# First modulation summed as columns, its last slot and the first w_in slot loaded in two parts, one MLP slot split around a norm

## Chip, cores and metric

The kernel runs on one core of one Trainium2 chip, as one program. The metric is the device time of an execution in microseconds (us); less is better. The profile is one execution, taken by the hardware profiler.

## What is computed

Two transformer blocks over 256 tokens (S) of width 1024 (D), all in float32. Only the first part is touched by the change:

```python
c_act = silu(c)                                  # 1 x 1024
mod = c_act @ w_ada + b_ada                      # 1 x 6144
sh1, sc1, g1, sh2, sc2, g2 = split(mod, 6)
h = rmsnorm(x, g[0]) * (1 + sc1) + sh1
y = token_mixer(h, w_in, w_out, sinks, bias)     # h @ w_in, attention, @ w_out
x = x + g1 * rmsnorm(y, g[1])
h = rmsnorm(x, g[2]) * (1 + sc2) + sh2
y = square(relu(h @ w1 + b1)) @ w2 + b2
x = x + g2 * rmsnorm(y, g[3])
...                                              # second block: mixer, then 16 experts
```

The second block ends with 16 experts, whose weights (w_gate, w_up, w_down, 24 MB an expert) are read once each.

## The kernel before, in words

Weights of everything ahead of the experts come through a ring of six slots of 1 MB (128 partitions x 2048 f32). `loads` lists them in order: eight slots of w_ada (`G_ADA0`, the columns of sh1 and sc1, slot k holding the rows p*8+k), nine of w_in (`G_WIN`), then w_out, the other w_ada slots, w1 and w2 (`G_MLP`), and the second block's. The sync queue (`block.sync`, L588) issues slot g when slot g-6 has been used; its semaphore is `loaded[g % 6]`. Other small loads stand in the same queue at fixed places: b_ada and b2 rows (L545, L547), the gain rows of w_ada (`load_gain`), the attention bias (L554). `tail_loaded` are three semaphores that the last unit of the last expert uses, hundreds of us later (L647, L1289). Experts' units of 4 MB go through a ring of five buffers laid over the same memory.

Order on every engine is written out by hand, and engines meet through semaphores.

The first modulation. `ada` (L776) takes one slot: four calls with `crep` (c_act of that slot, repeated to 32 columns) as the stationary operand and 512 columns of the slot as the moving one, each to its own 32 partitions of bank 2. So the sums lie in rows, one of 512 in each of four partition groups. After the third slot TensorE turns the eight 128x128 blocks of each of the two normalised token tiles (`turn_tiles`, through `turn`, L669); after the sixth, the rows of gains and biases and one product for the attention bias (L804). `turned_awake` (L733) are matmuls whose result nobody reads, two after each slot from the fourth on. VectorE copies the sums out in two halves (L1392), `turn_mod` (L785) turns them to columns with four calls, and `mod_columns` (L1375) adds b_ada; `fold_gain` multiplies the scale with the norm's gain. Then VectorE and ScalarE write the transposed, scaled and shifted tokens to `hT` (`place`; k 0 to 3 on VectorE, 4 to 7 on ScalarE, for tile 0, then tile 1).

The first w_in slot is used raw, in f32 (`raw_channels`, L745: 32 calls of 128x128 by 128 columns). All later slots are split: ScalarE writes a slot rounded to f32r (`round_slot`, L393), VectorE the rest (`residue_slot`, L403), both in two pieces, and the same is done to `hT` (`round_tile`, `residue_tile`, into `hR`). TensorE then takes three products of halves, in `both_still` (L722, L724) or `product` (L675 to L677).

Around the second norm (after w_out): x1 is summed per token tile (`first_sum`), ScalarE squares it (`root`, L1991), VectorE scales it (`norm_tile`, L1324), TensorE turns it, both place it. `G_MLP` is used raw, tile 0 then tile 1; `G_MLP + 1` is the first split slot. Before, both its pieces are rounded on ScalarE ahead of the square of tile 1 (L2118), and split on VectorE ahead of the norm of tile 1 (L1527).

## Time and profile before

| | us |
|---|---|
| median of 3 runs | 1452.87 |
| lowest and highest | 1452.32, 1454.32 |
| the profiled execution, device time | 1452.38 |
| its span (first to last instruction) | 1450.6 |
| TensorE busy (share) | 1060.3 (73%) |
| TensorE weight loads busy | 599.1 (41%) |
| VectorE, ScalarE, GpSimd busy | 425.8, 346.2, 85.8 |
| HBM read | 512.27 MB |

How to read it: the profiled execution's own time, 1452.38, is its span and 1.8 us around it. A line number (L787) is a line of the kernel; PE is TensorE, PEld its weight loads, DVE VectorE, ACT ScalarE, POOL GpSimd, SPq the queue of the sync engine that issues DMAs. A form such as 128x512 is partitions by elements. An f32 matmul call is recorded as two matmuls and two weight loads. "x8" is a count; what stands in brackets is the idle time before the group and what ended it. The times in a timeline start at the span's start.

### The profile page before, as it was taken

What the parts mean: (1) busy time and instruction counts of PE and PEld (TensorE: products, weight loads), DVE (VectorE), ACT (ScalarE), POOL (GpSimd) and SP (SyncE); (2) the same over time, 40 slices, a digit from 0 to 9 for tenths busy, and PEclk for the clock granted to TensorE, in tenths of its full rate; (3) what the DMA queues carried; (4) which work ended last, traced back from release to release, by engine and by line L of the source; (5) the groups of instructions that cost most, each with busy time, mean ns of one, the idle gap of its engine ahead of it and who ended that gap; (6) DMA issues with size and microseconds to landing.
All of it is one profiled execution on the core that took longest, in us unless ns stands there. A gap on an engine that the chain in (4) does not pass through costs nothing.

```text
span 1450.6 us, 15820 instructions
## 1 busy us (share of the span) xinstructions
PE 1060.3 (73%) x6734; PEld 599.1 (41%) x6734; DVE 425.8 (29%) x767; ACT 346.2 (24%) x600; POOL 85.8 (6%) x60
## 2 busy tenths in 40 slices
PE   6999999999999999766665565565545565655655
PEld 3866888888989985211211111121111121111111
DVE  3577776756979863000000000000000000000001
ACT  3566654636555942000000000000000000000001
POOL 1420059000000000000000000000000000000000
PEclk9999999999999999988888887788788878788788
DMA  9996468554564689999999999999999999999996
GB/s 362 338 376 205 147 230 262 191 186 146 175 232 125 261 342 418 431 431 430 428 432 432 432 431 430 432 431 430 429 431 432 433 433 428 431 429 431 433 432 279
DMA packets 83144, 514.50 MB, mean 355 GB/s; under 512 B 6659, under 2 KB 49134, under 8 KB 67330
## 3 DMA queue, kind: packets, MB, share of 16 engines
q1 hardware_dynamic: 82360, 512.68, 87.4%
q8 instruction: 53, 0.87, 0.3%
q10 hardware_dynamic: 490, 0.61, 0.1%
q0 software_dynamic: 224, 0.20, 0.0%
q14 instruction: 17, 0.14, 0.0%
HBM read 512.27 MB, written 1.07 MB: 354 GB/s over the span
## 4 chain that ended last, share of the span: by engine, by line
DMA 56%; PE 33%; DVE 7%; ACT 2%; issue 1%; SPq 1%; POOL 0%; DVEq 0%; ACTq 0%
DMA expert_ring<-in_w_up_e 20%; DMA expert_ring<-in_w_gate_e 18%; DMA expert_ring<-in_w_down_e 15%; PE PS L1255 6%; PE PS L675 5%; PE PS L677 5%; PE PS L676 5%; PE PS L722 4%; PE PS L724 2%; DVE wR L403 2%; PE PS L1294 2%; DMA ring<-in_w_in 1%; PE PS L749 1%; DMA ring<-in_w_ada 1%; ACT wR L393 1%
## 5 line engine op out<-in xcount | busy, mean ns | idle before, releaser
L1255 PE MATMUL PS<-expert_ring,xeT 128*32 128x512 f32 x2048 | 309.7, 761 | 225.9 <-DMA expert_ring<-in_w_up_e 124.0
L1255 PEld LDWEIGHTS PS<-expert_ring,xeT 128*32 128x32 f32 x2048 | 74.3, 135 | 458.1 <-issue 207.7
L1957 DVE TENSOR_TENSOR expert_rows<-expert_rows,PS 128x512 f32<-128x512 f32 x16 | 11.0, 687 | 805.6 <-PE PS L1255 805.6
L1294 PE MATMUL PS<-expert_ring,expert_rows 128*32 128x512 f32 x992 | 155.4, 777 | 103.7 <-DMA expert_ring<-in_w_down_e 101.4
L403 DVE TENSOR_TENSOR wR<-ring,wR 128x1024 fp32r<-128x1024 f32 x144 | 177.8, 1276 | 55.3 <-ACT wR L393 55.0
L393 ACT ACTIVATE wR<-ring 128x1024 fp32r<-128x1024 f32 x144 | 144.5, 1053 | 112.0 <-PE PS L677 110.8
L1294 PEld LDWEIGHTS PS<-expert_ring,expert_rows 128*32 128x32 f32 x992 | 38.7, 137 | 208.9 <-issue 119.5
L722 PE MATMUL PS<-hR,wR 128*128 128x512 f32 x320 | 112.2, 396 | 1.7 <-DVE wR L403 1.6
L724 PE MATMUL PS<-hR,wR 128*128 128x256 f32 x320 | 89.1, 278 | 0.0
L2332 ACT ACTIVATE selx<-PS 128x256 f32<-128x256 f32 x16 | 6.1, 384 | 322.4 <-PE PS L669 322.4
L675 PE MATMUL PS<-hR,wR 128*128 128x256 f32 x280 | 80.2, 286 | 0.8 <-DVE wR L403 0.8
L677 PE MATMUL PS<-hR,wR 128*128 128x256 f32 x280 | 79.2, 283 | 0.0
L676 PE MATMUL PS<-hR,wR 128*128 128x256 f32 x280 | 79.2, 283 | 0.0
L2327 ACT ACTIVATE expert_rows<-PS 128x512 f32<-128x512 f32 x16 | 9.6, 597 | 283.7 <-PE PS L1255 283.7
L2334 ACT ACTIVATE expert_rows<-PS 128x512 f32<-128x512 f32 x16 | 9.6, 597 | 257.0 <-PE PS L1294 257.0
L722 PEld LDWEIGHTS PS<-hR,wR 128*128 128x128 f32 x320 | 60.0, 188 | 16.5 <-issue 2.4
L724 PEld LDWEIGHTS PS<-hR,wR 128*128 128x128 f32 x320 | 60.2, 188 | 0.1
L675 PE MATMUL PS<-wR,hR 128*128 128x512 f32 (+1 forms) x144 | 55.7, 386 | 1.7 <-DVE wR L403 1.4
L677 PE MATMUL PS<-wR,hR 128*128 128x512 f32 (+1 forms) x144 | 54.3, 377 | 0.0
L676 PE MATMUL PS<-wR,hR 128*128 128x512 f32 (+1 forms) x144 | 54.3, 377 | 0.0
L675 PEld LDWEIGHTS PS<-hR,wR 128*128 128x128 f32 x280 | 53.7, 192 | 1.1 <-issue 1.0
L676 PEld LDWEIGHTS PS<-hR,wR 128*128 128x128 f32 x280 | 53.7, 192 | 0.0
(317 smaller groups left out, 1281.9 us busy)
## 6 DMA issues: line engine op xcount, KB each, us to landing
expert_ring<-in_w_down_e SPq DMA_DIRECT2D x30, 4096.0 KB, 44.2
expert_ring<-in_w_up_e SPq DMA_DIRECT2D x30, 4096.0 KB, 43.1
expert_ring<-in_w_gate_e SPq DMA_DIRECT2D x29, 4096.0 KB, 43.2
ring<-in_w SPq DMA_DIRECT2D x32, 1024.0 KB, 6.1
ring<-in_w_in SPq DMA_DIRECT2D x31, 1024.0 KB, 5.7
ring<-in_w_ada SPq DMA_DIRECT2D x16, 1024.0 KB, 12.8
ring<-in_w_out SPq DMA_DIRECT2D x8, 1024.0 KB, 10.6
expert_ring<-in_w_gate_e SPq DMA_DIRECT2D x4, 2048.0 KB, 12.4
```

The lines of the kernel that those rows point to most:

```text
L393: nc.scalar.activation(halves(g, 0)[:, piece], slot(g)[:, piece], ACT.Copy).then_inc(slot_rounded, 1)
L403: by.tensor_tensor(halves(g, 1)[:, piece], slot(g)[:, piece], halves(g, 0)[:, piece], ALU.subtract)\
L675: nc.tensor.matmul(o, first[0], second[0], start=start, stop=False, skip_group_check=onto)
L676: nc.tensor.matmul(o, first[0], second[1], start=False, stop=False, skip_group_check=onto)
L677: return nc.tensor.matmul(o, first[1], second[0], start=False, stop=stop, skip_group_check=onto)
L722: nc.tensor.matmul(o.rearrange("p (a s) -> p a s", a=2), w[0][:, k, cols], hR[:, :, k, :], start=(k == 0), stop=False, skip_group_check=True)
L724: mm = nc.tensor.matmul(o[:, 0:S], w[1][:, k, cols], hR[:, 0, k, :], start=False, stop=(k == KD - 1), skip_group_check=True)
L749: mm = nc.tensor.matmul(PS[:, bank, m * S + t * P:m * S + (t + 1) * P], k8(g)[:, k, m * P:(m + 1) * P], hT[:, k, t * P:(t + 1) * P], start ...
L1255: mm = nc.tensor.matmul(PS[32 * j:32 * j + 32, kind // 2, :], xeT[:, e // GROUP % 2, k, own], w[:, j // 2, j % 2, :, :], start=(k == 0), s ...
L1294: mm = nc.tensor.matmul(PS[32 * at:32 * at + 32, 3, :], hidT[:, c % 4, 2 * q + c // 4, :], w[c][:, 512 * half:512 * (half + 1)], start=(q ...
L1957: V.tensor_tensor(hid[:, :], silu[:, :], PS[:, 1, :], ALU.mult).then_inc(hid_set, 1)
L2327: N.activation(silu[:, :], PS[:, 0, :], ACT.Silu).then_inc(silu_set, 1)
```

## The change

1. `ada` is replaced for the first eight slots by `ada_columns`: the slot is the stationary operand, 16 blocks of 128x128, and c_act of that slot (one column) the moving one, into 16 columns of bank 2, summed over the eight slots. The copies to `modrow`, `turn_mod` for the first modulation and the `turned_awake` inside the loop go; `mod_columns` reads bank 2. The second modulation keeps its row form.
2. The eighth w_ada slot is loaded in two halves, with `tail_loaded[0]` for the first; the wait at the end of the kernel counts on from there.
3. The first w_in slot is loaded in two halves (k 0 to 3 and 4 to 7), and TensorE takes half by half, both token tiles of the first half first.
4. `G_MLP + 1`: the first piece is rounded and split ahead of tile 1's norm, the second behind it; VectorE places tile 1 ahead of splitting the tokens of tile 0.

```diff
@@ the sync queue
+                if g == G_ADA0 + 7:
+                    sp.dma_start(slot(g)[:, 0:D], ada_rows[7, :, 0:D]).then_inc(tail_loaded[0], 16)
+                    sp.dma_start(slot(g)[:, D:2 * D], ada_rows[7, :, D:2 * D]).then_inc(loaded[g % RING_P], 16)
+                    continue
+                if g == G_WIN:
+                    sp.dma_start(k8(g)[:, 0:4, :], src[:, 0:4, :]).then_inc(tail_loaded[1], 16)
+                    sp.dma_start(k8(g)[:, 4:8, :], src[:, 4:8, :]).then_inc(loaded[g % RING_P], 16)
+                    continue
                 sp.dma_start(dst(g), src).then_inc(loaded[g % RING_P], 16)
@@ TensorE
+            def ada_columns(k):
+
+                for c in range(2 * KD):
+                    if k == 7 and c == 0:
+                        pe.wait_ge(tail_loaded[0], 16)
+                    elif c == (KD if k == 7 else 0):
+                        arrived(pe, G_ADA0 + k)
+                    mm = nc.tensor.matmul(PS[:, 2, c:c + 1], slot(G_ADA0 + k)[:, c * P:(c + 1) * P], cact[:, k:k + 1],
+                                          start=(k == 0 and c == 0), stop=(k == 7), skip_group_check=True)
+                mm.then_inc(slots_used, 1)
 
             pe.wait_ge(crep_set, 1)
             for k in range(8):
-                ada(G_ADA0 + k, k, 2)
+                ada_columns(k)
...
-                if k >= 3:
-                    turned_awake(2)
 
             pe.wait_ge(bias_row_set, 1)
-            for part in range(2):
-                pe.wait_ge(modrow_set, part + 1)
-                turn_mod(0, 3, range(2 * part, 2 * part + 2))
             turned_awake(2)
-            arrived(pe, G_WIN)
-            for t in range(NT):
-                mm = raw_channels(G_WIN, 0, t, T1)
+            for half in range(2):
+                if half == 0:
+                    pe.wait_ge(tail_loaded[1], 16)
+                else:
+                    arrived(pe, G_WIN)
+                for t in range(NT):
+                    for j in range(4):
+                        pe.wait_ge(placed[half], placed_by(T1, t, j))
+                        k = 4 * half + j
+                        for m in range(2):
+                            mm = nc.tensor.matmul(PS[:, 0, m * S + t * P:m * S + (t + 1) * P], k8(G_WIN)[:, k, m * P:(m + 1) * P],
+                                                  hT[:, k, t * P:(t + 1) * P], start=(k == 0 and t == 0 and m == 0),
+                                                  stop=(k == KD - 1), skip_group_check=True)
             mm.then_inc(slots_used, 1)
...
-                                pe.wait_ge(tail_loaded[(c - 4) // 2 + c // 7], 16)
+                                pe.wait_ge(tail_loaded[(c - 4) // 2 + c // 7], 16 if c == 7 else 32)
@@ VectorE
             dve.wait_ge(slots_used, used(G_ADA0 + 7))
-            for part in (slice(0, S), slice(S, 2 * S)):
-                V.tensor_copy(modrow[:, 0, part], PS[:, 2, part]).then_inc(modrow_set, 1)
-            mod_columns(0, 3)
+            mod_columns(0, PS[:, 2, 0:16].rearrange("p (j q) -> p j q", j=4))
...
             first_sum(1)
-            residue_slot(dve, V, G_MLP + 1)
+            residue_piece(dve, V, G_MLP + 1, 0)
             norm_tile(N2, 1)
+            residue_piece(dve, V, G_MLP + 1, 1)
+            t2_place(1)
             residue_tile(T2, hT, 0)
-            t2_place(1)
             residue_tile(T2, hT, 1)
@@ ScalarE
             t2_place(0)
-            round_slot(act, G_MLP + 1)
+            round_piece(act, G_MLP + 1, 0)
             act.wait_ge(x1_set, 2)
             root(N2, 1, xres, ybuf)
+            round_piece(act, G_MLP + 1, 1)
             round_tile(T2, hT, 0)
```

## Rows read from the trace of the kernel before

**Rows 1.** The page: DMA share in 40 equal slices; the chain by engine.

```profile
DMA  9996468554564689999999999999999999999996
...
DMA 56%; PE 33%; DVE 7%; ACT 2%; issue 1%; SPq 1%; POOL 0%; DVEq 0%; ACTq 0%
```

**Rows 2.** Waits of the sync queue, 480 to 620 us: total us, times, longest.

```profile
SPq L597 <- DVE wR L403: 29.5, 5, 11.0
```

**Rows 3.** The chain in order of time, 0 to 45 us: start, us, what.

```profile
31.90 7.41 PE PS L749 x64
39.34 0.47 PE PS L722
```

**Rows 4.** Timeline of TensorE's matmuls: start, us, what, count [idle before].

```profile
9.31 1.94 PE L780 MATMUL PS<-ring,crep 128*32 128x512 f32 x8 [9.31 <-DMA ring<-in_w_ada]
...
16.44 1.97 PE L669 MATMUL PS<-const,work 128*128 128x128 f32 x16
18.34 1.06 PE L780 MATMUL PS<-ring,crep 128*32 128x512 f32 x8
...
23.44 0.38 PE L669 MATMUL PS<-const,arena 112*128 112x112 f32 x2
23.75 0.81 PE L804 MATMUL PS<-const,relb 32*16 32x384 f32 x2
...
27.46 1.07 PE L780 MATMUL PS<-ring,crep 128*32 128x512 f32 x8 [0.61 <-DMA ring<-in_w_ada]
```

**Rows 5.** Timeline of weight loads, 28 to 41 us.

```profile
29.13 0.97 PEld L787 LDWEIGHTS PS<-const,arena 128*128 128x128 f32 x8 [0.16 <-issue]
...
31.90 7.22 PEld L749 LDWEIGHTS PS<-hT,ring 128*128 128x128 f32 x64 [1.35 <-DMA ring<-in_w_in]
```

**Rows 6.** Stretches with clock, weight loads in 91.1:94.4 then 95:110, TensorE's timeline.

```profile
87.60:91.00 3.40, 1.23 (x12) 0.69 (x8) 2.27 (x5) 0.00 (x0) 0.50 (x1) 1.00 1.02 422
91.10:94.40 3.30, 3.27 (x16) 1.58 (x20) 2.55 (x4) 1.86 (x8) 0.00 (x0) 0.50 1.01 418
...
L857 PEld LDWEIGHTS PS<-arena 64*128 64x128 f32 x4 | 0.7, 333 | 0.2
...
L857 PEld LDWEIGHTS PS<-arena 64*128 64x128 f32 x20 | 1.9, 187 | 0.2
...
89.58 0.39 PE L857 MATMUL PS<-arena 64*128 64x128 f32 x4
...
92.15 0.64 PE L857 MATMUL PS<-arena 64*128 64x128 f32 x4
```

**Rows 7.** Timeline of VectorE, 28 to 40 us.

```profile
30.23 0.17 DVE L1378 TENSOR_TENSOR modcol<-PS,cols 128x16 f32<-128x16 f32 x1 [0.88 <-PE PS L787]
...
30.64 2.64 DVE L1339 TENSOR_SCALAR hT<-PS,fold,modcol 128x128 f32<-128x128 f32 x8
...
36.85 3.49 DVE L403 TENSOR_TENSOR wR<-ring,wR 128x1024 fp32r<-128x1024 f32 x3
```

**Rows 8.** Timelines of VectorE, ScalarE and TensorE, 148 to 159 us.

```profile
150.16 2.35 DVE L403 TENSOR_TENSOR wR<-ring,wR 128x1024 fp32r<-128x1024 f32 x2
...
152.62 0.75 DVE L1324 TENSOR_SCALAR work<-xres,stats 128x1024 f32<-128x1024 f32 x1
...
157.25 1.23 DVE L1350 TENSOR_TENSOR hR<-hT,hR 128x1024 fp32r<-128x1024 f32 x1 [1.46 <-ACT hR L2036]
...
150.60 1.06 ACT L1991 ACTIVATE ybuf<-xres 128x1024 f32<-128x1024 f32 x1
...
151.78 0.29 ACT L1993 ACTIVATE stats<-stats,eps 128x1 f32<-128x1 f32 x1
...
154.88 3.84 PE L749 MATMUL PS<-hT,ring 128*128 128x128 f32 x32 [0.36 <-DVE hT L1339]
```

**Rows 9.** Timeline of TensorE, six small transposes.

```profile
393.96 0.56 PE L669 MATMUL PS<-const,arena 36*128 36x36 f32 x6
```

**Rows 10.** DMA issues, 0 to 80 us: count, KB, median us to landing.

```profile
ring<-in_w_ada SPq DMA_DIRECT2D x13, 1024.0 KB, 12.8
```

More of the change, by code:

```diff
@@ L242, in build_program @@
         att_s = view(15104, HEADS, 8)
-        modrow = view(15232, 2, 512)
+        modrow = view(15232, 512)
         att_logits = hT[:, :, :].rearrange("p k s -> p (k s)")[:, 0:1536].rearrange("p (b h n) -> p b h n", b=2, h=2)
@@ L783, in ada, with turn_mod @@
                 mm.then_inc(slots_used, 1)
-            def turn_mod(r, bank, qs=range(4)):
-                for q in qs:
-                    mm = nc.tensor.matmul(PS[:, bank, 4 * q:4 * q + 4], modrow[:, r, q * P:(q + 1) * P], ident[:, 0:P:32],
+            def turn_mod(bank):
+                for q in range(4):
+                    mm = nc.tensor.matmul(PS[:, bank, 4 * q:4 * q + 4], modrow[:, q * P:(q + 1) * P], ident[:, 0:P:32],
                                           start=True, stop=True)
-                if 3 in qs:
-                    mm.then_inc(mod_turned, 1)
+                mm.then_inc(mod_turned, 1)
+            def ada_columns(k):
[7 more added lines that the diff above has]
+                mm.then_inc(slots_used, 1)
             pe.wait_ge(crep_set, 1)
             for k in range(8):
-                ada(G_ADA0 + k, k, 2)
+                ada_columns(k)
                 if k == 2:
@@ L908, in _ @@
                 if p == HEADS // 2:
-                    pe.wait_ge(modrow_set, 3)
+                    pe.wait_ge(modrow_set, 1)
                     wout(0, 0, range(2, 4))
@@ L921, in _ @@
                     pe.wait_ge(logit_set, HEADS // 2)
-                    turn_mod(1, 0)
+                    turn_mod(0)
                 if 1 <= p <= HEADS // 2:
@@ L1373, in _, with mod_columns @@
             V.tensor_tensor(logits[0:HEADS, 0, :], PS[0:HEADS, 3, 0:384], maskrow, ALU.add).then_inc(bias_row_set, 1)
-            def mod_columns(r, bank):
-                dve.wait_ge(mod_turned, r + 1)
-                V.tensor_tensor(modcol[:, r, :, :], PS[:, bank, 0:16].rearrange("p (q j) -> p j q", q=4),
+            def mod_columns(r, sums):
+                V.tensor_tensor(modcol[:, r, :, :], sums,
                                 colA[:, A_BADA + 24 * r:A_BADA + 24 * r + 16].rearrange("p (j q) -> p j q", j=4),
@@ L1470, in _ @@
                         dve.wait_ge(slots_used, used(G_ADA12 + 7))
-                        V.tensor_copy(modrow[:, 1, :], PS[:, 6, :]).then_inc(modrow_set, 1)
+                        V.tensor_copy(modrow[:, :], PS[:, 6, :]).then_inc(modrow_set, 1)
                 if p >= 3:
@@ L1478, in _ @@
             V.tensor_scalar(lam[:, 5:6], lam[:, 4:5], -LAM_INIT, None, ALU.add).then_inc(lam_set, 1)
-            mod_columns(1, 0)
+            dve.wait_ge(mod_turned, 1)
+            mod_columns(1, PS[:, 0, 0:16].rearrange("p (q j) -> p j q", q=4))
             fold_gain(1, 2, modcol[:, 1, 2:4, :].rearrange("p j q -> p (j q)"))
```

## Prediction

> **What bounds the kernel now.** I read the page first, then the chain of waits in order of time, then the timelines of the two stretches that the change touches. The page [rows 1] shows that from the 16th slice of 36.3 us on (544 us) the DMA share is 9 tenths, the last slice apart: the experts' weights stream, and the chain is DMA for 56%. That does not make the first 544 us free. The sync queue's waits around the start of the stream [rows 2] are on VectorE's splitting (29.5 us at L597) and on TensorE, so the stream starts when the stages before it have come far enough; after that it runs at a fixed rate. A microsecond gained or lost in a stage of the first 544 us moves the end by one microsecond, unless a stage between absorbs it. The chain of the first 40 us goes over the loads of w_ada and that of the first w_in slot, landed at 31.90, to 7.41 us of matmuls on it (L749) and to the long run of L722 from 39.34 [rows 3]. From there TensorE works without a gap until 56, so 39.34 is the mark: whatever moves the first L722 moves the rest.
>
> **Edit 1, the first modulation in column form.** Before, each of eight slots costs TensorE 4 calls, recorded as 8 matmuls of 512 columns in four column tiles that run side by side: 1.06 us, or 1.94 us for the first slot [rows 4]. It waits for DMA at most of them, and `turned_awake` fills in. Now a slot costs 16 calls with a 128x128 weight load each and one column moving. An f32 call is two records (L787: four calls, 8 records; L749: 32 calls, 64 records), so a slot is 32 pairs of weight load and matmul and the stage is 256. What is a pair worth? The nearest row is L787, 128x128 weights with 4 columns: 8 weight loads in 0.97 us, one lasting 0.19, so (0.97-0.19)/7 = 0.112 us per pair [rows 5]. L749 with 128 columns has (7.22-0.19)/63 = 0.112 as well [rows 5]: the moving columns do not set this, the weight load does, and one column will not be cheaper than four. A slot then costs 32 x 0.112 = 3.6 us where the loads come every (27.46-9.31)/7 = 2.6 us [rows 4]. The engine that waited for DMA becomes the limit: 256 x 0.112 = 28.7 us at the full clock.
>
> That is the price at 2.4 GHz. At 1.2 GHz it is more. The stretch 91.1 to 94.4 has a granted clock of 0.50 [rows 6]: there the 64x128 weight load of L857 takes 333 ns against 187 ns later, and its matmuls, two at a time, step by 0.64-0.42 = 0.22 us against 0.39-0.27 = 0.12 [rows 6]. That is 1.84 to 2 times, so a pair costs 0.206 to 0.224 us; I take 0.215, the middle. The Trainium skill (TensorE: Matmul & The Clock Gate, "LDWEIGHTS") gives a load as its columns over 1.2 and names no clock: 107 ns for 128 columns, which the 0.112 agrees with at 2.4 GHz. By it 1.2 GHz would cost nothing here and the stage would be 28.7 us; the 333 ns of L857 speaks against it.
>
> Which level holds? The kernel starts at 1.2 GHz: the first slot's L780 takes 1.94 us, that of 18.34 takes 1.06 [rows 4] (the clock column prints 1.00 there, for want of a record; the durations tell). What TensorE did before it rose, around 15.8 us, was 512-column matmuls from three slots. What it did before the fall at 91 was little: 1.23 us busy of 3.40 [rows 6]. In the changed stage TensorE loads weights nearly all the time and moves one column after each load. No stretch of this trace is like that; L787 is, and lasted 1.03 us inside other work. I judge it likelier that the stage stays at 1.2 GHz, because the rise that I can see stood behind wide matmuls and this work is of another kind; the other outcome is rival 1.
>
> The sum at 1.2 GHz: start 9.31 (first slot landed); 256 x 0.215 = 55.0; the 16 transposes after the third slot, 1.97 us at 2.4 GHz, 3.4 here (bounds 1.8 and 3.9); the turned rows and L804, 0.38+0.81 = 1.2, here 2.4 [rows 4]. Loads all land in time, the last of w_ada by 27.46, so no waits: the stage ends at 70.1. It ended at 28.5.
>
> Removed behind it: two copies and the four turning calls of L787. Before, 28.5 to the first placed tile at 30.64 is 2.1 us; now only the add and the fold remain, 30.64-30.23 plus a 0.04 hop = 0.45 [rows 7]. First place at 70.6. The gain of 1.7 us is in this.
>
> **Edit 2, the last w_ada slot in two loads.** One more issue, some 0.45 us on the sync queue, which waits there anyway. With TensorE the limit, an earlier half is of no use: nothing.
>
> **Edit 3, the first w_in slot by halves.** Same 64 pairs, two loads. Before, the slot landed at 31.90, 1.2 us after the first placed tile [rows 3, 7]. Now its issue waits for the third slot's use (about 30 us) and it lands near 40, long before 70.6: nothing again. The sync queue also holds the next w_in loads and the gain rows behind such waits; a load lands some 12.8 us after its issue (median) [rows 10], the last one that hangs on this stage is issued when it ends, and the slots are wanted one by one some 10 us later and more, so none is late. From first place to first L722 it was 39.34-30.64 = 8.70 us, with two paths equally long: 64 pairs, and placing, rounding, splitting on ScalarE and VectorE (to 36.85, then two pieces of 3.49/3 = 1.16) [rows 7]. At 1.2 GHz the pairs take longer until the clock rises. That took 3.3 us in the stretch at 91 [rows 6] and 6.5 us at the start, from 9.31 to 15.8 [rows 4]; half of it is lost, 1.6 to 3.2, I take 2.4. Then 0.35+7.3+2.4 = 10.05 us. First L722 at 80.65 against 39.34: **41.3 us later**.
>
> **Edit 4, the MLP's second slot around the second norm.** Before, ScalarE rounds two pieces ahead of its square of tile 1 (150.60), whose root is there at 151.78+0.29 = 152.07; VectorE splits two pieces in 2.35 us from 150.16, and scales at 152.62 [rows 8]. With one piece on either side, the square starts as soon as x1 is summed, about when VectorE takes the first piece: 0.35 us sooner. The root is there at 151.72, the scaling starts 0.2 later at 151.95, 0.67 sooner, and TensorE turns 0.67 sooner. VectorE then splits the second piece to 153.9 and places; it placed at 154.43, so 0.55 sooner. L749 of tile 1 starts at 154.3 instead of 154.88. What could be late next is the split of the tokens, now behind the placing: the last one starts 157.25 before and, bound by ScalarE, 0.7 to 0.8 sooner after, so it does not take over. Gain 0.6 us (bounds 0 and 0.8).
>
> **Total.** +41.3 - 0.6 = +40.7 us. The profiled execution took 1452.4 us (span 1450.6), 0.5 below the median of 1452.87. Forecast **1493 us**. Own range: 0.206 to 0.224 per pair is 52.7 to 57.3 us, and transposes, rows and the rise add 2 either way: 1489 to 1498.
>
> What could absorb it: between 73 and 89 us TensorE and VectorE wait for a chain of the sync queue (w_out, issued 72.88). Its issues hang on work of the w_in stage, which is late as a whole, so it moves along; at most 1 us comes back.
>
> **Rivals.**
> 1. The clock rises in the modulation stage. From 9.31 some 3.3 to 6.5 us at 1.2 GHz cost 1.6 to 3.2, take 2.4: 9.31+28.7+1.8+1.2+2.4 = 43.4; place 43.9; first L722 52.6, 13.3 late; less 0.6: +12.7, **1465 us** (1463.5 to 1467). For it: TensorE never pauses, and the fall at 91 stood behind pauses [rows 6]. Against: no row shows the clock rising behind work of this kind.
> 2. The column calls are no dearer than the loads (the other side). It decides at 2.6/32 = 0.081 us per pair: under that, the loads from HBM are the slower side again. Then the stage ends with the last load, 28.5; place 28.95 rather than 30.64, and w_in's first half is there for it: -1.7, with -0.6: **1450 us**. For it: six transposes with 36 columns take 0.56 us, (0.56-0.23)/5 = 0.066 each [rows 9]. The Trainium skill (TensorE: Matmul & The Clock Gate, "Back-to-back issue gap") likewise lists 1 to 64 columns at about 60 cycles, with 25 or 62 ns as the floor. Against: those transposes load weights at 0.14 us where an f32 product needs 0.19, and L787 with 4 columns is at 0.112.
> 3. The clock rises and falls within the stage, helped by the 16 transposes: between 1467 and 1489.
>
> **How the numbers follow.** Forecast 0.55; rival 1 0.30; rival 3 0.05; rival 2 0.06; unforeseen 0.04. The range goes from rival 1's low end to the forecast's high end, 1463 to 1498, and leaves out about one in ten. A measurement of this kernel tells 0.2% (2.9 us) from no change. Rival 2 is -2.3 us, so mostly within: same 0.06, faster 0.02, slower 0.92.
>
> **What would show it.** The line of `ada_columns` with 256 weight loads at a step near 0.21 us (forecast) or 0.112 (rival 1) and no DMA waits; the first placed tile near 70 or 44 us instead of 30.64; the MLP's L749 after a gap shorter by 0.6; the experts' stream unchanged in length. Wrong would be a TensorE that still waits for w_ada in that line, or pairs under 0.08 us, or a w_in stage that catches up what the first one lost.

## The result and the profile after

| | before | after |
|---|---|---|
| median, us (lowest to highest) | 1452.59 (1451.88 to 1454.32) | 1492.28 (1489.91 to 1492.34) |
| the profiled execution | 1452.38 | 1492.24 |
| its span | 1450.6 | 1490.4 |
| TensorE busy | 1060.3 | 1115.5 |
| TensorE weight loads busy | 599.1 | 653.8 |

The changed kernel is slower by 39.7 us, a ratio of 1.027 with a 95% interval of 1.0257 to 1.0282. The forecast was 1493 us, 40.7 us above before.

The page of the kernel after: the DMA share in 40 slices, the chain by engine, and the two groups of the new line (busy us, mean ns | idle before).

```profile
DMA  7579557755456478999999999999999999999996
...
DMA 53%; PE 36%; DVE 7%; issue 2%; ACT 2%; SPq 1%; POOL 0%; DVEq 0%; ACTq 0%
...
L806 PE MATMUL PS<-cact,ring 128*128 128x1 f32 x256 | 54.9, 352 | 9.3 <-DMA ring<-in_w_ada 9.3
...
L806 PEld LDWEIGHTS PS<-cact,ring 128*128 128x128 f32 x256 | 54.9, 333 | 10.5 <-issue 10.5
```

The slices are now 37.3 us long. The stream of the experts holds 9 tenths from the 17th of them on, where it did from the 16th [rows 1], and again to the end: the same stream, started later. The chain has 3 points more of TensorE. The new line, `ada_columns`, waits for a DMA once, 9.3 us for the first slot, and never again: the loads are no longer what this stage goes by. One weight load lasts 333 ns, which is to the nanosecond what L857 took while the granted clock was 0.50 [rows 6].

The timeline of TensorE after, to the first product on split weights (start, us, what, count):

```profile
9.26 20.61 PE L806 MATMUL PS<-cact,ring 128*128 128x1 f32 x96 [9.26 <-DMA ring<-in_w_ada]
29.73 3.65 PE L677 MATMUL PS<-const,work 128*128 128x128 f32 x16
33.17 20.48 PE L806 MATMUL PS<-cact,ring 128*128 128x1 f32 x96
53.51 0.54 PE L677 MATMUL PS<-const,arena 112*128 112x112 f32 x2
53.99 1.46 PE L822 MATMUL PS<-const,relb 32*16 32x384 f32 x2
55.37 13.81 PE L806 MATMUL PS<-cact,ring 128*128 128x1 f32 x64
69.05 1.20 PE L744 MATMUL PS<-const 128*128 128x128 f32 x4
70.19 8.45 PE L837 MATMUL PS<-hT,ring 128*128 128x128 f32 x64
78.40 0.49 PE L730 MATMUL PS<-hR,wR 128*128 128x512 f32 x1
```

VectorE after, around the first placed tile, and the largest group of waits of the sync queue between 520 and 660 us (total, times, longest):

```profile
69.22 0.17 DVE L1400 TENSOR_TENSOR modcol<-PS,cols 128x16 f32<-128x16 f32 x1 [13.12 <-PE PS L806]
...
69.63 2.65 DVE L1362 TENSOR_SCALAR hT<-PS,fold,modcol 128x128 f32<-128x128 f32 x8
...
SPq L605 <- DVE wR L403: 29.5, 5, 11.1
```

The first place stands 0.41 us behind the start of the add, as in [rows 7]. That group of waits at the head of the experts' stream is 29.5 us in all, as it was [rows 2]: the stream still waits for the stages ahead of it, so a late stage is a late end.

**How the lateness runs on.** The same VectorE instruction in both traces, start after less start before:

| where | before | after | later by |
|---|---|---|---|
| add of the first modulation | 30.23 | 69.22 | 39.0 |
| split of a w_out slot (L403) | 81.53 | 119.24 | 37.7 |
| softmax of a head pair (L1448, L1468 after) | 96.38 | 132.90 | 36.5 |
| reciprocal for tile 1 of the second norm | 152.43 | 188.57 | 36.1 |
| an early split in the MLP | 166.46 | 202.79 | 36.3 |
| first split beside GpSimd's work after | 199.99 | 237.25 | 37.3 |
| two slots on, the clock low between | 209.79 | 250.50 | 40.7 |
| two slots behind the late meeting of before | 262.28 | 301.43 | 39.2 |
| last hidden rows of the experts (L1957, L1979 after) | 1426.92 | 1466.55 | 39.6 |

So 2.5 us come back between 70 and 133 us, edit 4 gives some more, and 3.5 us are lost again in the MLP. The net is close to the 39.1 of the first stage, but not because nothing happened.

**What came back.** Before, ScalarE waited 1.0 us for the first w_out slot, and VectorE 1.45 for ScalarE:

```profile
80.37 2.01 ACT L393 ACTIVATE wR<-ring 128x1024 fp32r<-128x1024 f32 x2 [1.01 <-DMA ring<-in_w_out]
...
81.53 2.36 DVE L403 TENSOR_TENSOR wR<-ring,wR 128x1024 fp32r<-128x1024 f32 x2 [1.45 <-ACT wR L393]
```

After, the same split follows a wait of 0.36, and the lateness falls from 38.8 (the splits before it) to 37.7. The granted clock stays up in attention, where it fell to 0.50 before [rows 6]; there the lateness falls to 36.5 and ends at 36.8. VectorE's timeline and one stretch (columns: start:end, length, then busy us (count) of PE, PEld, DVE, ACT, POOL, granted clock, DMA share, GB/s):

```profile
119.24 2.36 DVE L403 TENSOR_TENSOR wR<-ring,wR 128x1024 fp32r<-128x1024 f32 x2 [0.36 <-ACT wR L393]
...
131.00:134.40 3.40, 2.82 (x30) 1.48 (x22) 3.33 (x9) 3.29 (x14) 0.00 (x0) 1.00 1.05 369
```

**What edit 4 did.** VectorE after, at the second norm:

```profile
186.94 1.22 DVE L403 TENSOR_TENSOR wR<-ring,wR 128x1024 fp32r<-128x1024 f32 x1
188.57 0.16 DVE L1342 RECIPROCAL stats<-stats 128x1 f32<-128x1 f32 x1 [0.41 <-ACT stats L2015]
...
189.59 1.23 DVE L403 TENSOR_TENSOR wR<-ring,wR 128x1024 fp32r<-128x1024 f32 x1
```

One piece stands on either side of the norm. The lateness goes from 36.78 (a softmax at 140.07, 103.29 before) to 36.14: 0.64 us sooner.

**What was lost again.** The MLP after, GpSimd's work on the second set of gain rows, VectorE's splits (the first by itself, then both), TensorE, and the clock:

```profile
237.12 1.35 POOL L2398 TENSOR_TENSOR ahead<-ahead 128x512 f32<-128x512 f32 x1
237.12 3.57 POOL L2398 TENSOR_TENSOR ahead<-ahead 128x512 f32<-128x512 f32 x2
...
237.25 2.32 DVE L403 TENSOR_TENSOR wR<-ring,wR 128x1024 fp32r<-128x1024 f32 x1
237.25 4.53 DVE L403 TENSOR_TENSOR wR<-ring,wR 128x1024 fp32r<-128x1024 f32 x2
...
241.92 0.47 PE L683 MATMUL PS<-wR,fR 128*128 128x512 f32 x1 [1.86 <-DVE wR L403]
...
243.10:246.50 3.40, 3.40 (x9) 2.64 (x9) 2.39 (x2) 0.00 (x0) 3.32 (x2) 0.50 0.83 334
```

And in the kernel before, the same two operations, then a pair of splits nine slots on and TensorE behind it:

```profile
199.99 2.35 DVE L403 TENSOR_TENSOR wR<-ring,wR 128x1024 fp32r<-128x1024 f32 x2
...
201.62 3.59 POOL L2375 TENSOR_TENSOR ahead<-ahead 128x512 f32<-128x512 f32 x2
...
249.68 4.53 DVE L403 TENSOR_TENSOR wR<-ring,wR 128x1024 fp32r<-128x1024 f32 x2
...
254.36 0.47 PE L722 MATMUL PS<-hR,wR 128*128 128x512 f32 x1 [1.57 <-DVE wR L403]
```

At 200 us of the kernel before, VectorE has both splits nearly done when GpSimd begins to add. After, GpSimd begins 0.13 us ahead of VectorE, and a split takes 2.3 us where it takes 1.2. The ends show turns: GpSimd's first addition ends at 238.47, VectorE's first split 1.10 later (239.57), GpSimd's second addition 1.12 after that (240.69), VectorE's second split 1.09 after that (241.78). TensorE waits 1.86 us for the split, and 1.2 us behind that wait its clock falls for 3.4 us. The Trainium skill (SBUF — State Buffer, "SBUF: two separate sides") says that VectorE with two inputs in SBUF and a GpSimd operation reading SBUF share a pair of ports under an exclusive lock, held for a whole instruction while the other blocks. The four ends agree with it; a mere sharing of bandwidth would have stretched all four instead of putting them in a row.

This meeting of the two engines is not the whole of the 3.5 us, and the kernel before is not free of it. Before GpSimd begins, the lateness has already grown from 36.1 to 36.9, by some 0.1 us a slot: the slots come every 5.65 us instead of 5.55, and the cause of that stays open. Across the meeting and the fall of the clock it goes to 40.7. Then the kernel before has a full meeting of its own (the splits at 249.68 take 4.53 us and TensorE waits 1.57), which brings the lateness back from 41.2 to 39.2, and 0.5 us come again by 0.1 a slot. So the meeting costs 2.3 us net of what the kernel before pays itself, and the slower slots 1.2.

### The profile page after: what moved, and what is told of

Same layout as the page of the kernel before. It is cut to its first block, busy times and chain, and to the rows that moved or that the text cites. A ratio compares the mean times of both kernels' runs of the same rounds, so it can differ in the third digit from the quotient of the medians.

```text
span 1490.4 us, 16148 instructions
## 1 busy us (share of the span) xinstructions
PE 1115.5 (75%) x6898; PEld 653.8 (44%) x6898; DVE 422.0 (28%) x765; ACT 346.0 (23%) x600; POOL 84.5 (6%) x60
## 4 chain that ended last, share of the span: by engine, by line
DMA 53%; PE 36%; DVE 7%; issue 2%; ACT 2%; SPq 1%; POOL 0%; DVEq 0%; ACTq 0%
DMA expert_ring<-in_w_up_e 20%; DMA expert_ring<-in_w_gate_e 17%; DMA expert_ring<-in_w_down_e 15%; PE PS L1278 5%; PE PS L683 5%; PE PS L685 5%; PE PS L684 5%; PE PS L730 5%; PE PS L806 4%; PE PS L732 2%; DVE wR L403 2%; PE PS L1317 2%; PE PS L677 1%; PE PS L837 1%; ACT wR L393 1%
## 5 line engine op out<-in xcount | busy, mean ns | idle before, releaser
L1278 PE MATMUL PS<-expert_ring,xeT 128*32 128x512 f32 x2048 | 321.1, 785 | 220.4 <-DMA expert_ring<-in_w_up_e 116.3
L1979 DVE TENSOR_TENSOR expert_rows<-expert_rows,PS 128x512 f32<-128x512 f32 x16 | 11.0, 688 | 805.7 <-PE PS L1278 805.7
L403 DVE TENSOR_TENSOR wR<-ring,wR 128x1024 fp32r<-128x1024 f32 x144 | 176.2, 1264 | 57.1 <-ACT wR L393 56.8
L730 PE MATMUL PS<-hR,wR 128*128 128x512 f32 x320 | 113.1, 398 | 0.0
L730 PEld LDWEIGHTS PS<-hR,wR 128*128 128x128 f32 x320 | 60.1, 188 | 14.6
L806 PE MATMUL PS<-cact,ring 128*128 128x1 f32 x256 | 54.9, 352 | 9.3 <-DMA ring<-in_w_ada 9.3
L732 PEld LDWEIGHTS PS<-hR,wR 128*128 128x128 f32 x320 | 60.5, 189 | 0.1
L806 PEld LDWEIGHTS PS<-cact,ring 128*128 128x128 f32 x256 | 54.9, 333 | 10.5 <-issue 10.5
```

The costliest lines, as they stand in the source:

```text
L403: by.tensor_tensor(halves(g, 1)[:, piece], slot(g)[:, piece], halves(g, 0)[:, piece], ALU.subtract)\
L730: nc.tensor.matmul(o.rearrange("p (a s) -> p a s", a=2), w[0][:, k, cols], hR[:, :, k, :], start=(k == 0), stop=False, skip_group_check=True)
L732: mm = nc.tensor.matmul(o[:, 0:S], w[1][:, k, cols], hR[:, 0, k, :], start=False, stop=(k == KD - 1), skip_group_check=True)
L806: mm = nc.tensor.matmul(PS[:, 2, c:c + 1], slot(G_ADA0 + k)[:, c * P:(c + 1) * P], cact[:, k:k + 1], start=(k == 0 and c == 0), stop=(k == ...
L1278: mm = nc.tensor.matmul(PS[32 * j:32 * j + 32, kind // 2, :], xeT[:, e // GROUP % 2, k, own], w[:, j // 2, j % 2, :, :], start=(k == 0), s ...
```

## The experiments

Theory A, that of the forecast: the stage costs 256 pairs, and one moving column behind each load leaves the clock at 1.2 GHz. Its rivals are that the pairs are dear for another reason than the clock, that the other edits matter, and that part of the 40 us is lost elsewhere. The kernels of before that ran beside them had medians of 1452.74 (for the first four), 1452.08 (the next four) and 1453.31 (the last three).

| kernel | median, us | ratio to before, 95% |
|---|---|---|
| columns_only | 1491.01 | 1.0261 (1.0246 to 1.0277) |
| mlp_only | 1451.91 | 0.9999 (0.9990 to 1.0008) |
| win_only | 1452.19 | 1.0000 (0.9991 to 1.0009) |
| rows_win_mlp | 1451.76 | 0.9998 (0.9990 to 1.0007) |
| wide128 | 1465.15 | 1.0085 (1.0070 to 1.0100) |
| wide64 | 1474.08 | 1.0149 (1.0133 to 1.0165) |
| wide32 | 1492.91 | 1.0276 (1.0259 to 1.0293) |
| delay39 | 1491.64 | 1.0272 (1.0254 to 1.0290) |
| pool_later_after | 1490.34 | 1.0258 (1.0243 to 1.0273) |
| pool_later_before | 1452.44 | 0.9996 (0.9987 to 1.0005) |
| hybrid | 1456.35 | 1.0026 (1.0018 to 1.0035) |

### Which of the four edits

**columns_only**: edit 1 alone; slots 7 and w_in's first come in one load, the MLP is as before.

```diff
-                ada(G_ADA0 + k, k, 2)
+                ada_columns(k)
```

> Edit 1 alone, the other three undone. Theory: the whole loss is edit 1's, so the time is that of the changed kernel give or take edit 4's 0.6 us: 1491 to 1494 us, pairs of L806 at 0.213 us, first w_in split slot at TensorE near 78.4 us. Rival (part of the loss, the 3 us that the MLP stage gives up between 237 and 255 us, is edit 4's): 1488 to 1490 us.

Measured: 1.0261, against 1.0270 for the whole change. Edit 1 is the change, as far as 1 to 2 us can be told. The rival had the loss in the MLP down to edit 4; it is out by the trace, for without edit 4 the two splits at 238.36 take 4.53 us as well. The trace holds one thing more. Stretches of columns_only:

```profile
33.00:36.30 3.30, 3.30 (x32) 3.30 (x31) 0.00 (x0) 0.00 (x0) 0.00 (x0) 1.00 0.39 135
36.50:70.40 33.90, 33.90 (x154) 32.22 (x155) 4.08 (x14) 3.90 (x10) 0.49 (x1) 0.50 0.60 202
```

Here the clock rose at 32.97, with the last of the 16 transposes (29.65 to 33.2 us), and fell again 3.4 us later, with TensorE busy all of the time on `ada_columns`. For those 3.3 us a pair costs 3.30/31 = 0.106 us; from then on it is 0.213 again, and the recorded clock is 0.50. This is rival 3 in small. In the kernel after, where TensorE's work is the same up to there, the transposes didn't raise the clock. The modulation of columns_only is 35.8 us late instead of 39.0, but its end, 39.2 us late, is not much sooner: it lacks edit 4, ScalarE waited 1.8 us for the first w_out slot, and the clock fell once more in its attention (128.5 to 132).

**mlp_only**: edit 4 alone.

```diff
-            residue_slot(dve, V, G_MLP + 1)
+            residue_piece(dve, V, G_MLP + 1, 0)
             norm_tile(N2, 1)
+            residue_piece(dve, V, G_MLP + 1, 1)
+            t2_place(1)
             residue_tile(T2, hT, 0)
-            t2_place(1)
...
-            round_slot(act, G_MLP + 1)
+            round_piece(act, G_MLP + 1, 0)
             act.wait_ge(x1_set, 2)
             root(N2, 1, xres, ybuf)
+            round_piece(act, G_MLP + 1, 1)
```

> Edit 4 alone. Theory: the MLP's second L749 group starts 0.5 to 0.6 us sooner than 154.88 and the time falls by 0.6 us (0 to 0.8). Rival (the order around the norm shifts VectorE against GpSimd's gain work near 200 us and they collide): 1 to 3 us slower than before.

**win_only**: edit 3 alone.

```diff
+                if g == G_WIN:
+                    sp.dma_start(k8(g)[:, 0:4, :], src[:, 0:4, :]).then_inc(tail_loaded[1], 16)
+                    sp.dma_start(k8(g)[:, 4:8, :], src[:, 4:8, :]).then_inc(loaded[g % RING_P], 16)
+                    continue
...
```

TensorE's part of the edit, half by half, is as in the change.

> Edit 3 alone, modulation in rows as before. Theory: the first matmul on the w_in slot starts some 0.9 us sooner than 31.90, but the first L722 waits for VectorE's splitting, which ends near 39.25, so it starts at 39.2 to 39.34 and the time is that of before within 0.2 us. Rival (TensorE is what L722 waits for): 0.5 to 1.2 us faster.

**rows_win_mlp**: edits 3 and 4 together, the row form kept.

> Edit 1 and its half load undone, edits 3 and 4 kept. Theory: before less 0.6 us, 1451.5 to 1452.3 us. Rival (edits 3 and 4 carry some of the loss): 1453 us or more.

Measured: none of the three differs from before; the best, rows_win_mlp, has an interval that reaches from 0.9990 to 1.0007. In the traces each does what it says. Across the second norm mlp_only's lateness goes from 1.91 to 1.28 us and that of rows_win_mlp from -1.45 to -2.08: 0.63 us gained in both, too little for the time to show. win_only starts its first L726 (L722 of before) at 39.51, 0.2 us later than before rather than sooner: TensorE begins on the slot at 31.37 instead of 31.90, but then waits 0.76 us for VectorE's split. In mlp_only, which loads the slot whole, it begins at 31.52 and waits 0.77, so little of even that half microsecond is edit 3's. The stretches that answer to the fall of the clock in [rows 6], first of mlp_only, then of win_only:

```profile
89.90:96.70 6.80, 5.63 (x28) 2.94 (x32) 4.20 (x8) 2.12 (x9) 0.00 (x0) 0.50 1.02 387
```

```profile
91.10:94.40 3.30, 3.30 (x32) 1.54 (x30) 3.23 (x8) 2.40 (x11) 0.00 (x0) 1.00 1.02 405
```

In a kernel that is the same as before up to there, the clock was low for 6.8 us; in the other it didn't fall. Before, it was low for 3.4. Between the first w_out split and the end of attention win_only gains 0.9 us on before and mlp_only loses 1.1, so such falls are worth about 1 us each way in a single profile, as much as edits 3 and 4 together, and they differ between kernels that differ by nothing at that place. A difference of under 2 us between two single profiles is therefore no evidence for an edit; the step of the lateness across the edit's own place is.

### How wide the moving side is

In all three, `ada_columns` moves c_act repeated, into as many columns of the sums, so that the loads and the number of pairs are the same.

```diff
-                    mm = nc.tensor.matmul(PS[:, 2, c:c + 1], slot(G_ADA0 + k)[:, c * P:(c + 1) * P], cact[:, k:k + 1],
-                                          start=(k == 0 and c == 0), stop=(k == 7), skip_group_check=True)
+                    mm = nc.tensor.matmul(PS[:, 1 + c // 8, 64 * (c % 8):64 * (c % 8) + 64], slot(G_ADA0 + k)[:, c * P:(c + 1) * P],
+                                          cact[:, k:k + 1].to_broadcast([P, 64]),
+                                          start=(k == 0 and c % 8 == 0), stop=(k == 7), skip_group_check=True)
```

That is **wide64**, in two banks; there `turned_awake` writes to another bank, and VectorE adds b_ada in two operations. **wide32** has 32 columns in one bank. **wide128** has 128 columns; sixteen such blocks don't go into a bank, so four blocks share each place, their sums are mixed, and what it computes from there on are other values in the same amount of work.

> The changed kernel with c_act repeated to 128 moving columns in each of the 128 calls, all in bank 2, so that the sums run into each other (the modulation's values are not the reference's; every operation is there). The weight loads are the same. Theory (a pair costs the weight load, and the clock falls with the kind of work): the clock rises within the first slots and pairs step at 0.112 us, the stage ends near 43 us, 1464 to 1467 us. Rival (dense weight loads keep the clock down, or cost the same whatever it is): pairs stay at 0.213 and the time at 1490 to 1493 us.

> 64 moving columns a call, in two banks, values right. If the clock rises as with 128, 1464 to 1467 us; if it stays down, 1490 to 1493 us. Theory: between, or one of the two, but not below the run with 128; the pair is 0.112 or 0.213 us, nothing in between but by the clock.

> 32 moving columns a call. Theory: weight load sets the pair, so 0.213 us at 1.2 GHz, and the clock stays down more of the time than with 64: 1480 to 1493 us. Rival (any wider moving operand raises it): 1464 to 1467 us.

TensorE's timeline of wide128:

```profile
9.60 13.45 PE L806 MATMUL PS<-cact,ring 128*128 128x128 f32 x96 [9.60 <-DMA ring<-in_w_ada]
22.90 1.91 PE L677 MATMUL PS<-const,work 128*128 128x128 f32 x16
24.64 10.88 PE L806 MATMUL PS<-cact,ring 128*128 128x128 f32 x96
...
52.92 0.47 PE L730 MATMUL PS<-hR,wR 128*128 128x512 f32 x1 [0.77 <-DVE wR L403]
```

of wide64:

```profile
9.13 20.72 PE L806 MATMUL PS<-cact,ring 128*128 128x64 f32 x96 [9.13 <-DMA ring<-in_w_ada]
29.64 3.29 PE L677 MATMUL PS<-const,work 128*128 128x128 f32 x16
32.77 10.83 PE L806 MATMUL PS<-cact,ring 128*128 128x64 f32 x96
```

and of wide32:

```profile
33.51 20.53 PE L806 MATMUL PS<-cact,ring 128*128 128x32 f32 x96
```

Measured: more columns make the stage cheaper. With 128 the clock rises at 14.85 us and a pair costs 0.112 to 0.113; the stage ends at 43.8 and the first L730 comes at 52.92. With 64, the first 96 pairs run at the low price for the whole 20.7 us, as with one column; then the clock rises at 32.46, within the transposes (29.64 to 32.93), and stays up: 96 pairs in 10.83 us. With 32 it is as with one: 0.213 throughout, 1492.9 us. The number of loads is the same in all of them, and TensorE was busy without a break from 9 us to the end of the stage in each. What changed is how much is moved behind each load. This is what theory A needs, and it excludes that the pair is dear by itself. All four runs of each kernel lie within 3.6 us of each other, so the outcome goes with the width and not with a single execution.

Three outcomes of one stage, then: a clock that rises at 14.85 us (128), one that doesn't rise on the pairs but stays up once it has risen in the transposes (64), and one that never rises in the stage (32, and one column in the kernel after) or falls again 3.4 us later (one column in columns_only). Other widths were not run.

### One column at the high clock

**hybrid** tries to gain: the row form for seven slots, the column form for the last alone, with edits 2, 3 and 4.

```diff
-            for k in range(8):
+            for k in range(7):
                 ada(G_ADA0 + k, k, 2)
...
                 turn_mod(0, 3, range(2 * part, 2 * part + 2))
+            for half in range(2):
+                ada_half(half)
             turned_awake(2)
```

> The change's other three parts, and the column form for the last of the eight slots alone: slots 0 to 6 are summed in rows, copied and turned while the last slot is on its way, and the 32 pairs of the last slot are added in column form to the turned sums. Theory (0.112 us a pair at 2.4 GHz, half of the slot landed 1 us before the other): 16 pairs, 1.8 us, stand behind the last load at 27.5, the first tile is placed near 29.8 instead of 30.64 and the first L722 comes near 38.5 instead of 39.34; with 0.6 us from the MLP slot 1451.1 to 1451.5 against 1452.6, a ratio of 0.999. Rival (copying and turning the seven slots' sums takes until 28 us and the pairs stand behind it, or the clock is low there): first tile at 30.6 or later, 1451.8 to 1453.

TensorE's timeline and two stretches of hybrid:

```profile
26.77 1.03 PE L808 MATMUL PS<-const,arena 128*128 128x4 f32 x8
27.65 4.12 PE L801 MATMUL PS<-cact,ring 128*128 128x1 f32 x32
31.63 1.20 PE L744 MATMUL PS<-const 128*128 128x128 f32 x4
32.77 9.69 PE L847 MATMUL PS<-hT,ring 128*128 128x128 f32 x64
```

```profile
27.60:30.30 2.70, 2.70 (x26) 2.70 (x25) 0.00 (x0) 0.00 (x0) 0.00 (x0) 1.00 1.10 354
31.10:34.50 3.40, 3.40 (x16) 3.19 (x16) 2.62 (x10) 2.23 (x7) 0.00 (x0) 0.50 1.08 351
```

Measured: slower than before, 1.0026, and slower than even the rival had it, so the theory fell, on two counts. The turning of the seven slots' sums ends at 27.7, when the last slot has landed, so all 32 pairs stand behind it and not 16: the first tile is placed at 32.22 instead of 30.64. And the clock, up since 17.1 us, fell at 30.78, 3.1 us into the one-column pairs, and stayed low for 6.8 us, which lies over the first w_in slot: its 64 pairs take 9.69 us instead of 7.41 [rows 3]. No pause comes before this fall. It is the plainest sight of the mechanism: with the engine busy throughout, the clock went down in work of this form, and the work behind it paid. (The profile is of the fastest of the 12 runs, 1454.0 us; what the slower ones lost besides is not on record.) The Trainium skill (TensorE: Matmul & The Clock Gate) says in "The HAM clock gate" that the clock is set by how busy the engine has been recently; by the records of matmuls and loads it was busy in every one of these stretches, so that sentence alone would have given rival 1, and the runs go against it. What the gate counts as busy can't be read from here.

The stretch 27.6 to 30.3 also gives a second price of a one-column pair at 2.4 GHz, 2.70/25 = 0.108 us.

### Whether lateness by itself costs or gives back

**delay39** is the kernel before with 174 more matmuls that nobody reads (348 records of 128 columns) ahead of the turned sums: late by as much as the change, with nothing of its form.

```diff
                 if k >= 3:
-                    turned_awake(2)
+                    turned_awake(2 if k < 7 else 176)
```

> The kernel before with 174 more unread matmuls of 128 columns behind its last w_ada slot: 174 x 0.224 = 39.0 us at 2.4 GHz, so that the w_in stage starts as late as in the changed kernel. Theory (lateness alone gives back 1 to 2.5 us in the attention and takes 1 to 3 us in the MLP stage): 1490 to 1493 us with the same pattern of shifts. Rival (the pattern comes from the column form): the shift of 39 stays the same through all stages, 1491.7 us, and VectorE's pieces near 240 us take 1.2 us each.

TensorE and VectorE of delay39:

```profile
28.55 39.57 PE L736 MATMUL PS<-const 128*128 128x128 f32 x352
```

```profile
236.94 4.53 DVE L403 TENSOR_TENSOR wR<-ring,wR 128x1024 fp32r<-128x1024 f32 x2
```

Measured: 1.0272, the same as the change. Its lateness is 38.7 at the modulation, 37.3 at the w_out slot and 36.1 to 36.4 in attention; in the MLP the splits at 236.94 take 4.53 us and the end is 38.2 late. So neither what came back nor what was lost again needs the column form: they are no further cost of `ada_columns`. That they go with being 39 us late is not shown, and other traces speak against it:

- columns_only and wide32 are as late, but the first w_out slot kept ScalarE waiting 1.8 us and the clock fell in attention for 3.4 us. Nothing came back there.
- win_only and rows_win_mlp are not late, and the clock stayed up in attention.
- hybrid, 0.4 us late at that place, has the full meeting (the splits at 200.84 take 4.52 us), and so have wide64, wide128, columns_only and wide32. TensorE waited 1.7 to 2.1 us behind it in all of them; only in the kernel after did the clock fall then. In delay39, without that fall, the lateness went from 36.4 to 38.8.

What decides between these outcomes no run here shows; each of them came at more than one lateness.

### The meeting of GpSimd and VectorE

**pool_later_after** and **pool_later_before** give GpSimd one more operation ahead of the first of the second gain rows, in the kernel after and in the kernel before.

```diff
                     pool.wait_ge(gain_loaded[k % 2], 16 * (k // 2 + 4))
+                    if k == 0:
+                        then(G.tensor_scalar(rows, rows, 1.0, None, ALU.mult))
```

> The changed kernel, with one more GpSimd operation (times 1.0, 128x1024, 2.85 us) ahead of the first of the second set of gain rows; nothing else moves. In the changed kernel VectorE's two splits at 237.25 take 4.53 us instead of 2.35, while GpSimd adds at 237.12, TensorE then waits 1.9 us and its clock falls for 3.4 us. Theory (two engines reading and writing at the same time; the lateness of the modulation brought them together): GpSimd's additions start near 240.0, the splits at 237 take 2.35 us, the clock doesn't fall at 243, the lateness stays near 36.5 until 250 us and the end comes 1.5 to 3.5 us sooner: 1489 to 1490.8 against 1492.3. Rival (the splits are slow for another reason, or the loss comes back in the next slots): splits still 4.5 us, or the same end within 0.7 us, 1491.6 to 1493.

> The kernel before with the same added GpSimd operation. There GpSimd's first additions stand at 201.62, between the splits at 199.99 (2.35 us) and those at 204.35 (3.08 us). Theory (it is the meeting alone that costs): they move to 204.5, on top of the splits at 204.4, which then take about 4.5 us, and the end comes 1 to 3 us later, unless ScalarE, for which VectorE waits there, hides it: 1453.5 to 1455.5. Rival (the meeting costs nothing where ScalarE sets the pace): 1452.1 to 1453.

GpSimd and VectorE of pool_later_after, and the stretch in which the clock fell in the kernel after:

```profile
236.71 3.95 POOL L2395 TENSOR_SCALAR ahead<-ahead,cact 128x1024 f32<-128x1024 f32 x1
...
236.82 3.18 DVE L403 TENSOR_TENSOR wR<-ring,wR 128x1024 fp32r<-128x1024 f32 x2
...
240.96 4.39 DVE L403 TENSOR_TENSOR wR<-ring,wR 128x1024 fp32r<-128x1024 f32 x2 [0.36 <-ACT wR L393]
...
243.10:246.50 3.40, 3.40 (x17) 2.82 (x16) 2.25 (x2) 0.55 (x1) 3.40 (x2) 1.00 0.68 218
```

and of pool_later_before:

```profile
203.65 4.39 POOL L2372 TENSOR_SCALAR ahead<-ahead,cact 128x1024 f32<-128x1024 f32 x1
...
207.03 3.46 DVE L403 TENSOR_TENSOR wR<-ring,wR 128x1024 fp32r<-128x1024 f32 x2 [1.63 <-ACT wR L393]
```

Measured, after: the splits take 3.18 us, not the 2.35 that I expected, beside GpSimd's multiplication (whose own time goes from 2.85 to 3.95); but that is 1.35 less than 4.53. The strict turns of the kernel after don't show here: the first split, begun 0.11 us behind the multiplication, took its usual 1.21 us. The meeting has moved on rather than gone, to the next pair of splits, which takes 4.39 us at 240.96. TensorE waits 0.44 us instead of 1.86 and the clock does not fall at 243. The lateness of the last hidden rows, 39.6 in the kernel after, is 36.8; of these 2.8 us, 1.6 are gained across the meeting. Most of the rest is slots that come every 5.55 us instead of 5.65, for which I have no cause. In the trace the theory holds in part. In the times it can't be decided: 1.0258 against 1.0270 is 1.8 us, and the intervals overlap (1.0243 to 1.0273, and 1.0257 to 1.0282).

Measured, before: no loss, 0.9996. The additions did not meet these splits in full, and where they did (3.46 us at 207.03) VectorE had waited 1.63 us for ScalarE, which sets the pace there; the delay went into that wait. So the second half of the theory is not confirmed. What the two fit is that the meeting costs where TensorE waits for the split, and nothing where VectorE has time to spare. (The profile here is of the slowest of the 12 runs.) What makes the gain row arrive earlier against VectorE I have only in part: its load takes 5.7 us from issue to landing in the kernel after and in hybrid, and 6.6 before.

## Why the prediction was right, point by point

**What bounds.** Right: the loss is made in the first stage, 39.1 us of lateness against 39.7 at the end, and the wait of the sync queue at the start of the stream is unchanged.

**Price and clock of a pair.** 0.213 against 0.215 forecast, and 54.9 us for the line against 55.0. The price at 1.2 GHz came from rows of another line at both clocks [rows 6], the price at 2.4 GHz, 0.112, from [rows 5]; columns_only and hybrid measured 0.106 and 0.108. The factor was a little better than its rows: 333 over 187 ns is 1.78 and 0.22 over 0.12 is 1.83, which gives 0.199 to 0.205, and no row gave the 2 of the upper bound. Measured, it is 1.9 to 2.0. By the Trainium skill (TensorE: Matmul & The Clock Gate, "LDWEIGHTS") a load of 128 columns is 107 ns, with no clock named; that agrees with a pair at 2.4 GHz and is half of a pair at 1.2.

**Which clock.** The likeliest case came, for the reason given (work of another kind than what raised the clock), and wide32, wide64 and wide128 turn that guess into a measurement. In the prediction it was an argument by likeness, with 0.55 on it. The argument for rival 1, that TensorE never pauses, does not hold: hybrid shows a fall without a pause.

**The other terms.** Transposes 3.65 (3.4 forecast), rows and product 2.0 (2.4), end of the stage 69.2 (70.1), first place 69.63 (70.6), 0.45 us behind the stage as forecast. The term that was mis-sized is the rise of the clock behind the stage: I took 2.4 us, half of an interval between the two that the rows showed, and the 64 matmuls took 8.45-7.41 = 1.0 us more than before, since the clock rose at 72.4, 2.2 us into them. The first L730 came at 78.40, not 80.65: 1.0 us of that error was there at the first place, and 1.3 came with this term.

**"At most 1 us comes back."** Wrong: 2.5 us came back, and the sum took none of it off. The w_out landing gave 1.1 of it, as I had allowed, and the w_in stage 0.2. The rest was in the fall of the clock at 91 us, which stood in my own rows [rows 6] as a price and which I did not count as something that a shifted schedule can lose or keep. The fall is not bound to the work there: the clock stayed up in after, win_only, delay39 and wide64, and was low for 3.4 us in before, columns_only and wide32 and for 6.8 in mlp_only.

**What I had not foreseen.** The 3.5 us in the MLP. No term of the sum had GpSimd's gain rows in it, nor slots that come 0.1 us slower; the prediction passes shifts on one to one. The sum had 2.3 us too many at L730 and none of the 2.5 that came back; it lacked the 3.5 lost in the MLP (36.1 to 39.6). These nearly cancel, by luck, and the forecast of 1493 against 1492.3 looks better than its steps are.

**Edit 4.** Right: 0.63 to 0.64 us in three traces against 0.6, and nothing late directly behind it.

**Edits 2 and 3.** Right that they bring nothing. For edit 2 there is no run of its own. For edit 3 the prediction named the reason, two paths of equal length; win_only shows the other path as a wait of 0.76 us for VectorE.

**The rivals.** Rival 1 did not come, but its sum was right for its case: 43.4, 52.6 and 1465 were forecast for a clock that rises early, and wide128 gives 43.8, 52.9 and 1465.2. Rival 3 came for 3.4 us in columns_only. Rival 2 needed pairs under 0.081 us; one-column pairs at the high clock cost 0.106, so it was out at any clock.

No kernel here beats the one before by more than can be measured; rows_win_mlp is level with it.

## What to carry to other kernels

A vector times a matrix that streams through once belongs in the form where the vector is the stationary operand and the matrix moves: here that was 1.06 us a slot against 3.6 for loading the matrix as weights at the high clock, and 6.9 at the low one that the second form brought with it. Price work of a form that the trace doesn't hold at both levels of the clock, and the work right behind it too: being busy was not enough here, neither for the pairs with 1 or 32 columns nor for the transposes after them, 3.65 us instead of 1.97. A run of the same loads with more moved behind each tells which level it is. A shift of a whole schedule passed to the end one to one only to within a few microseconds here: look for engines that meet by chance (VectorE and GpSimd with operands in SBUF) and for falls of the clock that a shift may add or remove, and read an edit's worth at its own place rather than at the end of one profile.

## What the runs showed of the hardware that I had not expected

- TensorE busy without a break for 60 us, on f32 weight loads of 128 columns with one or 32 columns moved behind each, stayed at 1.2 GHz (the kernel after and wide32). With 64 it did not raise the clock either, in 20.7 us, but kept it once transposes had been there; with 128 the clock rose at 14.85 us. The clock also went down during work with one column, 3.4 us behind its rise in columns_only and 3.1 us behind the start of the pairs in hybrid.
- Two VectorE splits with both inputs in SBUF and two GpSimd additions that began 0.13 us earlier took turns, instruction by instruction: 2.3 us each instead of 1.2 for VectorE, and 2.2 instead of 1.35 for GpSimd's second.
- The clock in the same stretch of attention was low for 0, 3.4 or 6.8 us in kernels that do not differ there, late ones and others alike.
